# A two-block transformer kernel, one core: the second block's matrix products take the residual times its norm weight, and the root mean square is multiplied in as the PSUM banks are emptied

## The reference, cut to what matters

```python
def _rmsnorm(x, g):
    y = xf * lax.rsqrt(jnp.mean(xf * xf, axis=-1, keepdims=True) + RMS_EPS)
    return (y * g.astype(jnp.float32)).astype(x.dtype)

def _sqrelu_mlp(h, w_up, w_down):
    a = jax.nn.relu(jnp.einsum('bld,df->blf', h, w_up))
    return jnp.einsum('blf,fd->bld', a * a, w_down)

for i in range(2):
    h = _rmsnorm(hres, norm_g[i, 0])
    # i = 0: differential attention, 8 heads; i = 1: gated short convolution
    m = _diff_attention(h, ...) if i == 0 else _short_conv(h, ...)
    hres = hres + _rmsnorm(m, norm_g[i, 1])
    h = _rmsnorm(hres, norm_g[i, 2])
    hres = hres + _rmsnorm(_sqrelu_mlp(h, w_up[i], w_down[i]), norm_g[i, 3])
```

## Time and profile before

| | |
|---|---|
| median of 3 runs | 2696.49 us |
| the profiled execution's own time, its span | 2697.29 us, 2695.5 us |
| PE busy, DVE, ACT, POOL | 93%, 48%, 40%, 19% |
| share of the chain that ended last on PE's matmuls | 65% |
| second block | from 1897 us to the end |

### The profile page before, as it was taken

One profiled execution on the slowest core, in us unless ns is written; L12 is line 12 of the kernel. 1 busy time (PEld: TensorE's weight loads), 2 busy tenths in 40 slices (PEclk: granted clock), 3 DMA queues, 4 the chain that ended last, 5 costly groups with the idle time before them and its releaser, 6 DMA issues.

```text
span 2695.5 us, 43581 instructions
## 1 busy us (share of the span) xinstructions
PE 2493.9 (93%) x19182; PEld 2415.3 (90%) x19182; DVE 1294.5 (48%) x1742; ACT 1075.4 (40%) x1590; POOL 508.4 (19%) x389
## 2 busy tenths in 40 slices
PE   5999988888799999999999999999876899997997
PEld 5999988888699999999999999999765799897997
DVE  5455364445544444444444444444544554455554
ACT  3332233324344444444444444444443454343542
POOL 1011232001112211221122122212100141022520
PEclk6787889889899999999999999999998899998999
DMA  6443122323245544444554554455311244342452
GB/s 235 157 157 125 64 94 88 112 92 121 87 172 176 182 174 174 180 179 172 178 182 173 174 185 174 172 177 183 109 69 47 79 173 173 140 148 103 172 188 79
DMA packets 55372, 392.09 MB, mean 145 GB/s; under 512 B 6032, under 2 KB 7696, under 8 KB 8080
## 3 DMA queue, kind: packets, MB, share of 16 engines
q1 hardware_dynamic: 54752, 387.83, 40.1%
q10 hardware_dynamic: 432, 1.49, 0.1%
HBM read 388.24 MB, written 1.05 MB: 144 GB/s over the span
## 4 chain that ended last, share of the span: by engine, by line
PE 65%; DVE 5%; ACT 2%; POOL 1%; issue 1%; DVEq 0%; ACTq 0%; POOLq 0%
PE ps L538 65%; ACT pp L1158 1%; DVE w_l L1642 1%; DVE pp L1648 1%; DVE st L1673 1%; ACT w_h L1158 1%; DVE R L1642 1%; DVE mxf L1648 1%; POOL H_l L2298 0%; DVE sms L2085 0%; DVE sms L1645 0%; DVE pp L1645 0%; ACT L1158 0%; DVE tf L1648 0%; PE ps L548 0%
## 5 line engine op out<-in xcount | busy, mean ns | idle before, releaser
L1642 DVE TENSOR_TENSOR w_l<-wraw,w_h 128x1024 fp32r<-128x1024 f32 x686 | 846.2, 1235 | 1034.4 <-ACT w_h L1158 1033.7
L1158 ACT ACTIVATE w_h<-wraw 128x1024 fp32r<-128x1024 f32 x686 | 723.5, 1056 | 862.6 <-PE ps L538 829.6
L538 PE MATMUL ps<-H_h,w_h 128*128 128x256 f32 (+1 forms) x3488 | 1030.5, 295 | 37.0 <-POOL H_l L2298 36.6
L538 PE MATMUL ps<-H_l,w_h 128*128 128x256 f32 (+1 forms) x3488 | 1006.4, 289 | 0.0
L538 PE MATMUL ps<-H_h,w_l 128*128 128x256 f32 (+1 forms) x3488 | 1006.2, 288 | 0.0
L538 PEld LDWEIGHTS ps<-H_h,w_h 128*128 128x128 f32 x3488 | 681.8, 195 | 69.1 <-issue 57.4
L538 PEld LDWEIGHTS ps<-H_l,w_h 128*128 128x128 f32 x3488 | 682.5, 196 | 0.1
L538 PEld LDWEIGHTS ps<-H_h,w_l 128*128 128x128 f32 x3488 | 682.5, 196 | 0.0
L538 PE MATMUL ps<-ar_h,w_h 128*128 128x256 f32 x1040 | 294.3, 283 | 0.0
L538 PE MATMUL ps<-ar_h,w_l 128*128 128x256 f32 x1040 | 294.2, 283 | 0.0
L538 PE MATMUL ps<-ar_l,w_h 128*128 128x256 f32 x1040 | 294.1, 283 | 0.0
(11 more groups left out here) (255 smaller groups left out, 2719.8 us busy)
## 6 DMA issues: line engine op xcount, KB each, us to landing
wraw<-in_w_in SPq DMA_DIRECT2D x66, 1024.0 KB, 4.8
wraw<-in_w_eg SPq DMA_DIRECT2D x64, 1024.0 KB, 4.8
wraw<-in_w_eu SPq DMA_DIRECT2D x64, 1024.0 KB, 4.7
wraw<-in_w_ed SPq DMA_DIRECT2D x64, 1024.0 KB, 4.8
wraw<-in_w_up SPq DMA_DIRECT2D x32, 1024.0 KB, 4.8
wraw<-in_w_down SPq DMA_DIRECT2D x32, 1024.0 KB, 4.8
wraw<-in_w_ada SPq DMA_DIRECT2D x24, 1024.0 KB, 4.8
wraw<-in_w_out SPq DMA_DIRECT2D x12, 1024.0 KB, 4.8
```

The costliest lines, as they stand in the source:

```text
L538: return e.matmul(o, a, b, start=start, stop=stop, skip_group_check=skip)
L1158: return e.activation(o, i, f, **kw)
L1642: return e.tensor_tensor(o, a, b, op)
```

## The change

1. ACT writes the high part of R x weight straight from R as soon as a tile of R is there (`high_of`, the weight as the activation's scale). The low part is R x weight - high: DVE makes it for tiles 0, 2, 4, 6 between its residual additions, POOL for 1, 3, 5, 7 in two instructions (`low_of`). The 1/rms is not waited for.
2. PE makes the first three halves side by side (`three`): for each k, nine matmuls into three banks. Then the fourth, then the eight sums of squares that stood ahead of the products before. ACT's squares and root come after the splits for the halves 4 to 6 behind the first.
3. 1/rms comes in when a bank is emptied. In the mlp, DVE multiplies the bank by 1/rms, DVE then squares the relu, and ACT makes `X_h`. q, k and the convolution's outputs are emptied by DVE, v by ACT with 1/rms as a column, which PE transposes for it (`rv`).
4. The second block's ring has six banks.
5. DVE's split of the fourth half of the next weights (`advance`) stands ahead of its residual additions.

```diff
+LOWS = ["PPPPPPPP"] * 2 + ["DPDPDPDP"] * 4
...
+RING = [0, 1, 2, 3, 6, 7]
...
 # PE
+            def three(us, outs, inst, c):
+                for k in range(KB):
+                    w.wait_ge(*HLV[inst, k])
+                    for u, o in zip(us, outs):
+                        w.wait_ge("wl", u + 1)
+                        t = mm3(o, blk(u, k), hx(k, c), k == 0, k == KB - 1)
+                        if k == KB - 1:
+                            w.then_inc(t, "used", USED[u])
...
+            def first_heads():
+                w.wait_ge("rm", 8)
+                us = [HALF["w_in2", 4 * j] + m for j in range(2) for m in range(2)]
+                three(us[:3], [head_bank(n)[:, 0:L] for n in range(3)], HI["att"], ALLT)
+                w.then_inc(proj(us[3], head_bank(3)[:, 0:L], HI["att"], 0, 8, ALLT), "used", USED[us[3]])
                 for k in range(KB):
                     sum_squares("r2", k)
+                values(0, 0)
+                w.wait_ge("rcp", 1)
+                for i, (q0, nq) in enumerate(QT):
+                    t = tr(ps[2][0:nq, i * P:(i + 1) * P], STD[SI["r2"] % 2][:, q0:q0 + nq])
+                w.then_inc(t, "rcol")
+                values(0, 1)
+                values(0, 2)
...
 # ACT
+            def high_of(inst, c, gcol, sem, base):
+                for k in range(KB):
+                    w.wait_ge(sem, base + k + 1)
+                    w.then_inc(act(H[0][:, k, c], R[:, k, c], ACT.Copy, scale=gcol(k)), "hh", 8 * inst + k + 1)
...
             def mlp(layer):
-                to_h(HI[f"mlp{layer}"], c)
...
-                for b in range(32):
-                    h = HALF["w_up2", 16 * layer + b // 2] + b % 2
-                    advance(h)
-                    if b:
-                        high(b - 1)
-                    if 32 * layer + b >= 3:
-                        w.wait_ge("xl", 32 * layer + b - 2)
-                    w.wait_ge("used", USED[h])
-                    w.then_inc(act(MF[(32 * layer + b) % 3][:, 0:n], ps[EV2["u", layer, b][0] % 4][:, 0:n], ACT.Relu), "relu", 32 * layer + b + 1)
-                high(31)
+                advance(hs[0])
+                high_of(HI[f"mlp{layer}"], c, lambda k: n2[:, 4 * layer + 2, k:k + 1], "rx", 16 * layer)
+                for b in range(1, 4):
+                    advance(hs[b])
+                mean_square(f"a{layer}", ALLT)
+                advance(hs[4])
+                for b in range(32):
+                    if b > 4:
+                        advance(hs[b])
+                    w.wait_ge("sqr", 32 * layer + b + 1)
                     w.then_inc(copy(X2[0][:, b, c], MF[(32 * layer + b) % 3][:, 0:n]), "xh", 32 * layer + b + 1)
...
 # DVE
             def add_mix(...):
...
                     w.then_inc(tt(R[:, k, c], R[:, k, c], f, ALU.add), "rx", base + k + 1)
+                    if inst is not None and k:
+                        w.wait_ge("rx", base + k)
+                        low_of(inst, k - 1, c, gcol)
...
             def mlp(layer):
+                for b in range(1, 5):
+                    advance(hs[b])
+                x = rstd(f"a{layer}")[:, L - n:L]
                 for b in range(32):
-                    advance(h)
+                    if b > 4:
+                        advance(hs[b])
...
-                    w.wait_ge("relu", 32 * layer + b + 1)
-                    w.then_inc(tt(f, f, ps[i % 4][:, 0:n], ALU.mult), sem, v)
+                    w.wait_ge("used", USED[hs[b]])
+                    if q >= 3:
+                        w.wait_ge("xl", q - 2)
+                    w.then_inc(tt(f, ps[RING[i % len(RING)]][:, 0:n], x, ALU.mult), sem, v)
+                    w.wait_ge(sem, v)
+                    w.then_inc(stt(f, f, 0.0, f, ALU.max, ALU.mult), "sqr", q + 1)
...
             def conv_in():
+                    w.wait_ge("used", USED[us[b]])
+                    w.then_inc(tt(BCU[:, 8 * j + 2 * p + m, :], ps[RING[i % len(RING)]][:, 0:L], x, ALU.mult), sem, v)
...
 # POOL
+            def low_of(inst, c, gcol, src, base):
...
+                        w.chain(e.tensor_scalar(f, R[:, k, c], gcol(k), None, ALU.mult))
+                        w.settle()
+                        w.wait_ge("hh", 8 * inst + k + 1)
+                        w.then_inc(tt(H[1][:, k, c], f, f32(H[0][:, k, c]), ALU.subtract), sem, v)
```

More of the change, by code:

```diff
@@ L144, with low_counts @@
 HI = {"mix": 0, "ffn": 1, "att": 2, "mlp0": 3, "conv": 4, "mlp1": 5}
+LOWS = ["PPPPPPPP"] * 2 + ["DPDPDPDP"] * 4
+def low_counts():
+    at, out = {"D": 0, "P": 0}, {}
+    for i, by in enumerate(LOWS):
+        for k, q in enumerate(by):
+            at[q] += 1
+            out[i, k] = ("hl" + q, at[q])
+    return out
+HLV = low_counts()
 FIRST = []
@@ L1415, in moe, with values, first_heads @@
                 advance(dn + 1)
[L1416 to L1420, removed]
+            def values(p, i):
+                u = HALF["w_in2", 8 + p]
+                nq, n = QT[i][1], 7 * p + 4 + i
+                w.wait_ge("vz", 3)
+                if i < 2:
+                    w.wait_ge("vv_pe", 2 * p + i + 1)
+                else:
+                    w.wait_ge("used", USED[u])
+                w.then_inc(act(VV[0:nq, i, p * 256:(p + 1) * 256], ps[n % 2][0:nq, 0:256], ACT.Copy, scale=rv[0:nq, i:i + 1]), "ph_act", 3 * p + i + 1)
+            def first_heads():
+                us = [HALF["w_in2", 4 * j] + m for j in range(2) for m in range(2)]
+                advance(us[0])
+                high_of(HI["att"], ALLT, lambda k: n2[:, 0, k:k + 1], "rm", 0)
+                for u in us[1:]:
+                    advance(u)
+                mean_square("r2", ALLT)
+                u = HALF["w_in2", 8]
+                advance(u)
+                w.wait_ge("rcol", 1)
+                w.chain(copy(rv[0:16, 0:1], ps[2][0:16, 0:1]))
+                w.then_inc(copy(rv[:, 1:3], ps[2].rearrange("p (i c) -> p i c", i=4)[:, 1:3, 0]), "rvc", 1)
+                w.settle()
+                w.wait_ge("rvc", 1)
+                for i in range(3):
+                    values(0, i)
+                advance(u + 1)
             def project_heads(p):
@@ L2136, in mixer_out @@
                             square(name, b, MT[:, b, :])
-                add_mix(name, 4 * layer + 1, ALLT, 16 * layer)
+                advance(HALF["w_up2", 16 * layer])
+                add_mix(name, 4 * layer + 1, ALLT, 16 * layer, HI[f"mlp{layer}"], lambda k: n2[:, 4 * layer + 2, k:k + 1])
             def mlp(layer):
@@ L2408, in mlp @@
                 n = L - META if layer else L
-                to_h(HI[f"mlp{layer}"], c)
+                low_of(HI[f"mlp{layer}"], c, lambda k: n2[:, 4 * layer + 2, k:k + 1], "rx", 16 * layer)
                 for b in range(32):
```

298 lines of the change are left out of this document (157 added, 141 removed).

## The result

The changed kernel takes 2710.34 us (median of 9 runs, 2703.28 to 2715.14), the kernel before 2697.55 us (median of 9, 2689.13 to 2700.3). The ratio is 1.0055, with a 95% interval from 1.004 to 1.0071: slower by 0.55%, about 15 us by the ratio and 12.8 by the medians. The forecast was 2726 us, with a range from 2706 to 2744.

What follows compares the result with a forecast made beforehand. It took PE's matmuls, broken by attention and the four entries, to bound the second block. Heads 7, attention 2, first mlp 15.6 - 4.7, convolution -4.9, second mlp 20.0 - 5.7 made +29.3: 2726 us, range 2706 to 2744.

Steps and rivals of the forecast that it cites:

- The loop: In both mlps ACT and DVE wait for each other: 3.57 and 3.53 us per half, against PE's 3.03 and 2.84.
- the squaring of the relu: In the mlps, DVE's squaring on SBUF within each half's chain of waits, put at 0.50 us like `mxf`.
- the stall of 1.0 to 1.4 us at the start: At half 8 PE runs out of prepared weights: 1.0 us lost in the first mlp, 1.4 in the second.
- The ring's loss: Mutual waits of ACT and DVE, including the initial stall, cost 15.6 us in the first mlp and 20.0 in the second.
- The entries: Starting products before 1/rms wins 4.7 us net at the first mlp, 4.9 at the convolution, 5.7 at the second mlp.
- The slow clock: At the entries PE's first products after idling run at half clock, taken as 7 us long, between 4 and 9.
- the second and the third rival: Second: entries at full clock, 2711 us, chance 0.13. Third: DVE and POOL shut each other out, 2735 us, chance 0.17.
- Heads: At the heads' entry the first attention step comes 7 us later, the lambda chain having lost its cover.
- Attention: Moving q and k to DVE, where softmax runs, and v to ACT costs 2 us.
- I take 2: In attention, the 2 us chosen as the cost of moving q and k to DVE, from between 0 and 6.
- the band of 2715 to 2731: Whole kernel: time range of the likeliest case, the forecast with its sizes, given chance 0.60.
- The sum: Whole kernel: all terms together +29.3 us, 2726.6 for the profiled execution and 2726 for a median of runs.

Runs made afterwards that it cites:

- the opened kernel: The changed kernel with ACT's split of half b+3 moved ahead of the copy X_h of half b in both mlps: 2681.69 us, ratio to before 0.9948.
- the lambda chain: The changed kernel with the lambda products and their exponential moved ahead of the first heads: 2711.12 us, ratio to before 1.0046.
- the swap: The kernel before with only q and k emptied by DVE and v by ACT in the head pairs: 2698.66 us, ratio 1.0014.

## Why the prediction was right, and where it was not

- **The loop.** Right as a mechanism: forecast 3.57 and 3.53 us, measured 3.50 and 3.46. The terms that were too large are the squaring of the relu, put at 0.50 from `mxf`, which took 0.44 with one SBUF input, and the stall of 1.0 to 1.4 us at the start. The ring's loss was forecast at 15.6 and 20.0; opening it gave 12.7 and 17.3. In the first mlp 27 x (3.50 - 3.03) = 12.7 leaves nothing for the stall: the copies are 3.50 us apart from the sixth half on.
- **The entries.** Before less the opened kernel gives 6.5 us for the first mlp, 5.5 for the convolution and 6.3 for the second mlp, against 4.7, 4.9 and 5.7. The slow clock was put at 7 us of PE's work. The 0.57 from 2142 to 2145 puts its end near 2144.6, 3.3 us after PE's first product at 2141.34; it was 5.7 in the convolution and 3.5 in the second mlp, the rest fell into PE's idle time. The last of the 72 matmuls ended 14.0 us after the first `mxf` instead of 14.8. POOL's last low part came at 12.6, not 10.2, since DVE and POOL stretched each other. So the mechanisms of the second and the third rival are both there: the clock rose earlier, the tiles came later, and the two errors nearly cancel. That part of the agreement is luck.
- **Heads.** +7 was forecast and +8.4 measured. The forecast took 1898.15, which is the start of the sums, for the end of PE's last half, which is 1897.68; from there its first product was due after 7.5 us and came after 7.86. The table load did stand ahead of the last square, at 1913.60. Moving the new split behind the additions gave 1.8 us here, the lambda chain 1.2. Of the 1.4 us by which the sum was short, 0.4 lie ahead of that first product; where the other 1.0 lie is open.
- **Attention.** +2 against +7.0. The step "I take 2" was too low by 1.2 by the swap alone; of the rest it is known that the clock was lower, and that a difference of this size also comes without any edit there.
- **The experts** are the step that is missing from the sum: it has no term for what stands ahead of the second block, as if what the change does not edit stayed as it was, while the diff allocates a buffer ahead of the experts'. With that undone the kernel takes 2717.54 us, in the band of 2715 to 2731.
- **The sum.** 2697.29 + 29.3 = 2726.6; less 10.2 for the experts and what is ahead of them and 1.6 for all else (+1.4, +5.0, -4.7, 0, -3.3) is 2714.8, against the profiled 2715.14. That profiled execution is the slowest of nine, 4.8 over its median, where 0.8 was assumed. The second block's 27.7 for 29.3 is partly luck: errors of 6.4 and 8.0 us cancel.

## What to carry to other kernels

Before giving an engine a new wait, write down the ring: if A's next piece stands behind what waits for B, and B's work behind what waits for A, the pace is the sum of all steps, though both helpers are idle for a good part of it. One swap in the order, the next split ahead of the copy, was worth 29 us. A split whose result is needed late belongs behind the instructions that PE waits for. After adding a buffer look at the addresses of the others, and before comparing two kernels at the level of half a per cent, compare the stages that neither edit touches.

## What the hardware showed beyond this

- Moving the experts' activations by 32 bytes took their matmuls from 283 to 280 ns and an expert from 17.90 to 17.73 us; 64 bytes made it 17.80. At a granted clock of 1.00 this is worth 0.3% of the kernel.
- DVE's scalar_tensor_tensor on two SBUF tiles took 0.49 to 0.50 us alone and 0.73 to 1.01 with POOL at work, and POOL's scaling of the same width 1.14 to 1.48.
- The attention stretch took 193.5 us at a granted clock of 0.89 in one kernel and 199.5 at 0.85 in another, without an edit in it. Such a stage hides differences of a few us, and a single profile cannot size them.
